# VectorE masks a chunk's scores ahead of scaling the outputs of the chunk in front, and makes its two low halves behind the last gated output

## What is computed

```python
cq, ckv_raw, kpe_raw, gq, gk, gv, glr, gr, ga, gb = split_cols(rmsnorm(x) @ w_in)
o_a = mla_attention(...)                       # latent attention, 8 heads
o_g, s_new = gla(qg, kg, vg, la, s0)           # gated linear attention, 4 heads, 128 x 256 state
o_b = rmsnorm(o_g, g_gla_norm) * silu(gr)
merged = sigmoid(ga) * (o_a @ w_branch_a) + sigmoid(gb) * (o_b @ w_branch_b)
x = x + merged @ w_out
x = x + hier_moe(rmsnorm(x), ...)              # 32 experts, 2 per token
```

```python
qe = q * exp(bcum); ke = k * exp(-bcum)
att = where(causal, qe @ ke.T, 0)
o = qe @ s + att @ v
s_new = exp(b_last) * s + (k * exp(b_last - bcum)).T @ v
```

## Time and profile before

| | us |
|---|---|
| median of 3 runs | 1073.99 (1073.92 to 1075.62) |
| profiled execution, its own time | 1074.43 |
| its span | 1072.6 |
| TensorE busy | 978.6 (91%) |
| VectorE busy | 392.2 (37%) |
| ScalarE busy | 282.4 (26%) |
| GpSimd busy | 210.3 (20%) |
| granted TensorE clock, mean | 0.966 |

### The profile page before, as it was taken

How to read it: one execution, slowest core, us unless ns; L and a number is a source line. 1 busy time by engine, 2 the same in 40 slices (tenths; PEclk the granted TensorE clock), 3 DMA queues, 4 the chain that set the end, 5 groups by cost and what they waited for, 6 DMA issues and landing times.

```text
span 1072.6 us, 15247 instructions
## 1 busy us (share of the span) xinstructions
PE 978.6 (91%) x6278; PEld 682.8 (64%) x6278; DVE 392.2 (37%) x764; ACT 282.4 (26%) x486; POOL 210.3 (20%) x121
## 2 busy tenths in 40 slices
PE   9999999999999999999998999779888777987885
PEld 6997888889988999999994333333333333333332
DVE  7275844433886524213434111111111111111118
ACT  5435445454566621222213000000000000000012
POOL 0332122223312444343210011110110111001000
PEclk9999999999999999999999999999898889999898
DMA  9342521222111332532758999999999999999993
GB/s 234 86 92 83 183 60 40 60 80 61 50 50 31 108 99 81 171 89 81 314 238 335 398 427 425 426 426 428 428 427 427 427 428 427 426 426 428 424 410 148
DMA packets 108943, 267.56 MB, mean 249 GB/s; under 512 B 21821, under 2 KB 88797, under 8 KB 95666
## 3 DMA queue, kind: packets, MB, share of 16 engines
q1 hardware_dynamic: 104178, 258.06, 62.9%
q0 software_dynamic: 4704, 8.64, 2.1%
HBM read 256.12 MB, written 18.17 MB: 256 GB/s over the span
## 4 chain that ended last, share of the span: by engine, by line
PE 59%; DMA 27%; DVE 7%; issue 3%; ACT 2%; POOL 1%; SPq 0%; DVEq 0%; POOLq 0%; ACTq 0%
PE proj L1086 33%; DMA we<-in_w_exp_up 25%; PE proj L1560 11%; PE proj L1576 3%; PE bank L1237 2%; DMA zc<-expert_out 1%; PE bank L1264 1%; PE bank L1250 1%; PE bank L1456 1%; DMA expert_out<-yo,sidx 1%; DVE x_rows L2706 1%; DVE xsT L2633 1%; PE bank L1586 1%; PE proj L1206 1%; ACT ex L1916 1%
## 5 line engine op out<-in xcount | busy, mean ns | idle before, releaser
L1560 PE MATMUL proj<-we,xsT 128*64 128x512 f32 x512 | 250.2, 646 | 68.5 <-DMA we<-in_w_exp_up 62.2
L1562 PE MATMUL proj<-we,xsT 128*64 128x512 f32 x512 | 250.6, 647 | 0.0
L949 POOL TENSOR_TENSOR wlo<-raw,whi 128x1024 fp32r<-128x1024 f32 x68 | 156.9, 2308 | 377.0 <-PE proj L1086 353.9
L1560 PEld LDWEIGHTS proj<-we,xsT 128*64 128x64 f32 x512 | 73.2, 149 | 211.7 <-issue 196.4
L1086 PE MATMUL proj<-hT_hi,whi 128*128 128x272 f32 x688 | 147.1, 295 | 2.5 <-POOL wlo L949 1.4
L1086 PE MATMUL proj<-hT_hi,wlo 128*128 128x272 f32 x688 | 145.3, 293 | 0.0
L1086 PE MATMUL proj<-hT_lo,whi 128*128 128x272 f32 x688 | 145.0, 292 | 0.0
L2625 DVE TENSOR_TENSOR hg<-hg,proj 64x512 f32<-64x512 f32 x32 | 22.1, 690 | 308.9 <-ACT hg L2072 295.8
L2072 ACT ACTIVATE hg<-proj 64x512 f32<-64x512 f32 x30 | 17.7, 590 | 424.0 <-PE proj L1562 424.0
L1576 PE MATMUL proj<-we,hT 128*64 128x512 f32 x256 | 115.2, 593 | 2.0 <-DVE hT L2628 1.1
L1577 PE MATMUL proj<-we,hT 128*64 128x512 f32 x256 | 115.2, 593 | 0.0
(11 more groups left out here) (394 smaller groups left out, 1385.7 us busy)
## 6 DMA issues: line engine op xcount, KB each, us to landing
we<-in_w_exp_gate SPq DMA_DIRECT2D x31, 2048.0 KB, 32.2
we<-in_w_exp_up SPq DMA_DIRECT2D x31, 2048.0 KB, 36.7
we<-in_w_exp_down SPq DMA_DIRECT2D x31, 2048.0 KB, 38.8
raw<-in_w_in SPq DMA_DIRECT2D x43, 512.0 KB, 3.9
x_rows<-in_x_prompt SPq DMA_DIRECT2D x8, 512.0 KB, 4.7
raw<-in_w_branch_b SPq DMA_DIRECT2D x8, 512.0 KB, 4.1
raw<-in_w_out SPq DMA_DIRECT2D x8, 512.0 KB, 4.2
zc<-expert_out SPq DMA_DIRECT2D x4, 1024.0 KB, 17.4
```

The costliest lines, as they stand in the source:

```text
L949: nc.gpsimd.tensor_tensor(lo[:, 0:c], raw[n % NRAW][:, 0:c], hi[:, 0:c].bitcast(F32), ALU.subtract).then_inc(w_split, 1)
L1560: pe.matmul(proj[0:SLOTS, s, 0, :], xsT[:, k, cols], wg[:, k * FF:(k + 1) * FF], start=(k == 0), stop=(k == KD - 1))
L1562: mm = pe.matmul(proj[64:64 + SLOTS, s, 0, :], xsT[:, k, cols], wu[:, k * FF:(k + 1) * FF], start=(k == 0), stop=(k == KD - 1))
```

## The change

In the loop over chunks `masked(c)` no longer opens iteration c; `masked(c + 1)` stands in iteration c between `branch(0, c)` and `normed_output(c)`. Behind the loop the wait for `last_ot` and the gated output of the last chunk stand ahead of the two low halves instead of behind them.

```diff
         for c in range(NT):
             if c:
-                masked(c)
-            if c:
                 new_state(c - 1)
...
                 decayed(c + 1)
                 branch(0, c)
+                masked(c + 1)
                 normed_output(c)
...
         branch(0, 4)
+        dve.wait_ge(last_ot, 1)
+        gated_output(NT - 1, [bank[:, 1, n * P:(n + 1) * P].rearrange("p (h l) -> p h l", l=DEC) for n in range(2)])
+
         for h in range(EARLY_LOW, GH):
             dve.wait_ge(ob_high, h + 1)
             part = output_part(h)
             v.tensor_tensor(ob_lo[part], gqk[part], ob_hi[part].bitcast(F32), ALU.subtract).then_inc(ob_ready, 1)
-        dve.wait_ge(last_ot, 1)
-        gated_output(NT - 1, [bank[:, 1, n * P:(n + 1) * P].rearrange("p (h l) -> p h l", l=DEC) for n in range(2)])
-
         dve.wait_ge(ob_ready, GH)
```

## The result

The change makes the kernel slower. Measured beside the kernel before on the same chip, its median is 1079.37 us (12 runs, 1078.03 to 1083.06) against 1075.12 (12 runs, 1073.62 to 1077.51); the ratio is 1.0045, 95% interval 1.0035 to 1.0054, which is + 4.8 us (3.8 to 5.8). Four single executions, of 1387.95 to 3979.45 us, lie far above all others, one of the kernel before, two of "one turn" and one of "gaps filled", and count in no ratio. Forecast were + 4.0 and 1078.0. The profiled execution took 1080.27 us, 5.84 more than that of before (0.90 of it from ahead of anything that moved).

The account below looks back on a forecast made before the run. TensorE was taken to bound the stretch of chunks; + 5.4 us there and - 1.4 in the tail gave + 4.0 on 1074.43, 1078.4, or 1078.0 on the median's scale; range 1073.2 to 1079.6.

Parts of the forecast that it names:

- Step 1, chunk 1: Mask ahead of scaling: transposes L1340 0.8 us earlier, but GpSimd's split holds the last exponent; L2407 2.5 us late.
- Step 2, chunk 2: The split again goes in ahead of or between the last two exponents; L2407 and the output products L1413 5.95 us late.
- Step 3, chunk 3: Chunks 3 and 4: L1340 5.4 us late, chunk 4 covers VectorE's further delay; the stretch ends 5.4 late.
- Step 4, the tail: Low halves behind the last gated output: GpSimd's split no longer late, 1.4 us gained; the new wait costs nothing, by 0.8.
- the term of the clock: Rival, 8%: TensorE's clock falls in the new gaps of chunks 1 and 2, 1.6 us each; 1079.6 or 1081.2.
- one for one: Gains or losses in the gated-linear-attention chunks carry unchanged through the expert stage to the kernel's end.
- The turn is missed in chunk 1: Rival, 20%: the last exponent op gets in before GpSimd's split; stretch 3.1 us late, + 1.75 in all, 1075.7.
- No turns paid: Rival, 20%: only VectorE's order delays the stretch, 0.9 us late against 1.4 won; - 0.5, 1073.5.
- The waits just vanish: Rival, 10%: TensorE's 2.2 us of mask waits go, all but 0.6, plus 1.4 in the tail; - 3.0, 1070.9.
- who goes first: Weak point, chunk 1: GpSimd's split, asked for at 303.85, goes ahead of VectorE's exponent op at 304.1.

Follow-up runs that it names:

- one turn: Changed kernel, but only GpSimd's split of tile ga 2 waits for VectorE's exponents; 1077.78 us against 1075.12 for the kernel before, ratio 1.0016.
- gaps filled: Changed kernel plus TensorE products on constants during its L2407 waits in chunks 1 and 2; against the kernel before, six: ratio 1.0055, three: 1.0022.
- mask alone: Kernel before with only the mask moved, low halves still ahead of the last gated output; 1083.2 us against 1074.65, ratio 1.0077.
- second profile: The changed kernel, unaltered, run once more for another profile; 1082.25 us in a single run.
- tail alone: Kernel before with only the low halves moved behind the last gated output; 1072.91 us against 1074.65, ratio 0.9979.
- kernel without turns: Changed kernel, but GpSimd's splits of tiles ga 2 and ga 3 wait for VectorE's exponents; 1073.67 us against 1074.65 for the kernel before, ratio 0.9985.

## Why the prediction was right and where it was wrong

*Step 1, chunk 1: right.* Lined up, the mask starts at 296.33 (forecast 296.28), L1340 at 297.08 (297.0), the state copy at 298.29 (298.25), the last exponent operation at 304.14 (304.1), the split asks at 303.91 (303.85), and L2407 starts at 306.89 (307.0).

*Step 2, chunk 2: right in kind, 1.5 us short.* The split again gets in, ahead of the last two operations. But lined up chunk 2's L1326 is at 318.61, where the sum had 295.13 + 19.47 + 2.5 = 317.1. With the gaps filled it is 21.82 us behind chunk 1's, and the sum had 21.97. The clock's fall makes the rest.

*Step 3, chunk 3: right but for the clock.* L1340 was due at 341.4 and is at 344.58 lined up. With the gaps filled, chunk 3's scores are 44.16 us behind chunk 1's, forecast 339.56 - 295.13 = 44.43. The short chunk 4 absorbed VectorE's delay, as forecast: L2407 of chunk 3 still waited 2.35 us for TensorE.

*Step 4, the tail: right, a little better.* GpSimd's halves 4.74 us (4.8), no wait behind them, VectorE's branch product 5 starts 8.01 us ahead of L2400 of the first branch-b product, against 12.34 before, and ends at 389.70, 1.0 us before the first product that reads the low halves (390.69): still in time, forecast 0.8. The profile shows 1.6 us gained from chunk 4's scores to that L2400; by the runs the tail is worth 2.3 us (1.2 to 3.4), forecast 1.4.

**The step that failed** is the term of the clock, which the sum left at nothing: "Here the products around the gaps are dense, so I leave it a rival", with 8%. The clock fell in both gaps, in both profiles of the changed kernel and in that with the mask alone, and once in that with one turn. The price of 1.6 a time was right for the shorter falls (1.7 measured; the two longer ones, in the second profile and in that with one turn, cost about 3.0), the chance was not: it belonged in the sum, which would have been + 5.4 + 3.2 - 1.4 = + 7.2. By the stretch and the tail, + 8.55 - 1.6, that is what the profile shows at the first branch-b product (396.99 lined up is 396.09, before 389.16: + 6.9). The Trainium skill, TensorE: Matmul & The Clock Gate, HAM oscillation — how this bites in real kernels, states, for a loop that waits for its DMA between groups of matmuls, that the next group starts at the lower clock. This case's trace agrees that the clock falls around such a wait: 3.03 us of waiting, then 0.59 of the full clock over the next 4 us. It does not agree on the place each time: of the seven falls two begin inside the wait and five behind it, between 0.2 and 1.3 us after TensorE has resumed.

That the median is nonetheless + 4.8 and near the forecast is luck: two misses against each other. From the first branch-b product's L2400 to the end, the profiled executions take 683.4 us before and 681.4 after; 1.7 of these 2.0 lie between the first two experts, where before the clock fell and after it did not. So the carry "one for one" is the second step that did not hold. The profiles on record say more of this place. VectorE's product L2625 of the first two experts, in the kernel before and in that with the tail alone:

```profile
587.96 0.69 DVE L2625 TENSOR_TENSOR hg<-hg,proj 64x512 f32<-64x512 f32 x1 [7.60 <-ACT hg L2072]
598.84 0.69 DVE L2625 TENSOR_TENSOR hg<-hg,proj 64x512 f32<-64x512 f32 x1 [8.92 <-ACT hg L2072]
```
```profile
588.87 0.69 DVE L2625 TENSOR_TENSOR hg<-hg,proj 64x512 f32<-64x512 f32 x1 [7.60 <-ACT hg L2072]
598.06 0.69 DVE L2625 TENSOR_TENSOR hg<-hg,proj 64x512 f32<-64x512 f32 x1 [7.22 <-ACT hg L2072]
```

They are 10.88 us apart in both kernels with the old tail (before, mask alone) and 9.18 or 9.19 in all eight profiles with the new one, where the granted clock stays at 1.00 between them. Against this, five of the eight take 1.1 us longer up to the first expert than the kernel before, three do not (198.8 us). So the tail seems to move where the clock falls in the expert stage, and the forecast has no term for it; with one or two profiles of a kernel, and no run made for it, this is an observation and its cause stays open.

*The rivals.* "The turn is missed in chunk 1" did not happen: requests 0.23 and 0.05 us ahead of the next operation's start were enough (304.81 against 305.04, 328.29 against 328.34). "No turns paid" did not happen by itself; the kernel without turns enforces it, and its 0.9 us in the stretch are those of this rival's sum. "The waits just vanish" failed at the place named, L2407. On who goes first, the rule of the Trainium skill (SBUF — State Buffer, Who interferes with whom) held: the split that asked first ran whole, 2.52 and 2.34 us, and the operation that started second ended 0.54 us behind it.

## What to carry to other kernels

An operation moved earlier on one engine moves what its consumer triggers on a third. Here an earlier mask brought GpSimd's split forward while the wait in front of it pushed VectorE's exponents back, and the two closed a gap of 0.4 us in one chunk and none in the next. Before reordering VectorE, list GpSimd's operations on SBUF beside it with their triggers, and put into the time in which an engine will wait something that is ready, as the state update here (it undid the mask's loss, and gained no more than the tail alone). In this kernel each of the seven new waits of 3.0 to 3.5 us on TensorE went with a fall of its clock, at 1.7 us or more, and the waits of 0.9 to 1.3 us with none; a new wait of that length should carry the price of a fall in the sum. And two moves in one change should be priced, and run, apart: here one gained 2.3 us and the other lost 8.3.

## What the runs showed that I had not expected

- The fall's length changes from one execution to the next at the same place: about 3.4 us at half clock in one profile of the changed kernel, about twice that in the other, after the same wait of 3.03 us.
- A fall can come without a wait of TensorE. In the kernel without turns the clock fell at about 364.8 us, just behind the last chunk's small products, with TensorE busy throughout. It is the only one of the ten profiles in which this happened there, and it cost that execution 1.5 us:

```profile
364.50:367.90 3.40, 3.40 (x17) 3.40 (x18) 2.27 (x6) 3.37 (x6) 0.00 (x0) 0.54 0.65 203
```

- With waits of 0.89 and 1.31 us in chunks 1 and 2 that kernel kept its full clock there.
- Operations with two operands in SBUF are not the only ones that a GpSimd split holds. In the kernel before, the cap L2328, with one such operand and a constant, takes 1.23 us when nothing meets it; started while a split ran it took 2.21, and so at this place in the other profiles:

```profile
280.47 1.35 POOL L949 TENSOR_TENSOR wlo<-raw,whi 128x512 fp32r<-128x512 f32 x1 [7.54 <-PE proj L1086]
280.70 2.21 DVE L2328 TENSOR_SCALAR ex<-ex 128x2048 f32<-128x2048 f32 x1
```
